# Splitting weight tiles of 2048 columns into halves of 1024 between ScalarE, VectorE and TensorE

## The chip, the cores and the metric

The kernel runs on one core of one Trainium2 chip. The metric is the device time of one execution in microseconds. Engines are named as the profile names them: PE is TensorE (PEld its weight loads), DVE is VectorE, ACT is ScalarE, POOL is GpSimd and SP is SyncE.

## The reference

Two transformer-like blocks run one after the other, in f32, for one sequence of 512 tokens with D = 2048 (the first block has two layers, with a second stream of 256 context tokens). Cut to what matters here, every layer is a chain of products of the activations with large weight matrices, and smaller work between them:

```python
hl = xl * (1.0 + sc_l) + sh_l                 # modulation, from silu(c) @ w_mod
parts = jnp.split(hl @ w_in[l], SPLIT_POINTS) # 2048 x 8192
y = concat(short_conv(...), diff_attention(...), multiscale_pool(...))
x = layernorm(ALPHA * x + gate * (y @ w_out[l]))
# second block: the same frame, with
y_attn = banded_sink_attention(q, k, v, ...) * silu(g_attn)
u = glu_a * sigmoid(glu_b)                    # then a causal depthwise conv of 31 taps
y_conv = (silu(layer_norm(u)) @ w_pw + b_pw) * silu(g_conv)
```

## The kernel before, in words

**Weight tiles.** All large products are cut into 296 weight tiles. A tile holds the 128 output columns that one PSUM bank receives, for all 2048 inputs: in SBUF it is 128 partitions x 2048 columns, of which each block of 128 columns is one stationary operand. The tiles are numbered through the whole program (`j`), and the list `STREAM` gives their order: for the context tokens `cconv`, `chead`, `cpool`, `cout` (tiles 0 to 71, 256 tokens), for the main tokens `aconv` to `aout` (72 to 143, 512 tokens), `kv1` (144 to 159, 256 tokens), `bconv` to `bout` (160 to 231), then the second block: `glu` (232 to 255), `kv2`, `attn2`, `pw`, `out2` (to 295), with 512 tokens.

**Three terms.** An f32 product is made of three passes: the weights and the activations are each split in a rounded part and a rest (`hi`, `lo`), and PE adds hi*hi + hi*lo + lo*hi. So a tile takes 48 matmuls (lines 946 to 948 in `product`, 16 blocks of 128 inputs times 3).

**The path of one tile.** SP loads `raw` (1 MB) when the rest of tile j-2 is written (`load`, line 350, waits for `lo_done`). ACT copies it rounded to `w_hi` (`hi`, line 542; the instruction is recorded at the helper's line 540) when the load has landed and PE has finished tile j-2 (`tile_done`). DVE writes `w_lo` = `raw` - `w_hi` (`lo`, line 1270, instruction at line 1274). PE waits for `lo_done` at the head of `weight_tile` (line 951). `raw`, `w_hi` and `w_lo` hold two tiles each, by the parity of j, and there are two PSUM banks for results (`acc`, freed by `acc_free`).

**The order on each engine** is written out by hand. ACT's stream in every stage is: `hi(j + 1)`, then the eviction of tile j when PE has finished it. So `hi(j + 1)` always stands behind the eviction of tile j-1. DVE's stream is: `lo(j + 1)`, then the stage's own work on earlier results. That work is small in some stages and large in others: in `aconv` and `bconv` DVE also multiplies modulation weights of the next layer (`mod_tiles`, line 1321) whose tiles POOL loads, in `aconv` and `kv1` it finishes the layer norm of the stage before (lines 1586, 1594, 1605, 1611), and in `glu` and `kv2` it computes the 31 taps of the depthwise convolution (`taps`, line 1731, instruction at 1739), about 10 taps behind each `lo`. At the head of each stage ACT and DVE first make the activations' `h_hi` and `h_lo`; PE follows block by block through the stage's first tile (`split_before`), and the second tile's `hi` stands behind that work on ACT.

**A tile in two results.** In `pw` a weight tile holds two products of 8 blocks each; the first signalled `pw_done`, the second `tile_done`.

`shown(sem, n)` gives the value of a semaphore when n events have happened, counting what it was granted at the start; `At` is a linear expression in the loop's counter.

Of the kernel before, what the change touches and what calls it, by code (L numbers as in the profile page):

```python
# [8 lines left out]
F32 = mybir.dt.float32  # L9
F32R = mybir.dt.float32r  # L10
ALU = mybir.AluOpType
# [4 lines left out]
D = 2048  # L16
KT = D // P
# [91 lines left out]
def build(nc, A, out):  # L109
    with ExitStack() as ctx:  # L110
        def sb(name, cols, dt=F32, rows=P):
            return ctx.enter_context(nc.sbuf_tensor(name, [rows, cols], dt))

        def psum(name, cols):
            return ctx.enter_context(nc.psum_tensor(name, [P, cols], F32))
# [3 lines left out]
        def sem(name, credit=0):  # L119
            s = ctx.enter_context(nc.semaphore(name))  # L120
            credits[id(s)] = credit
            return s
# [5 lines left out]
        raw = sb("raw", 2 * D)  # L128
        w_hi = sb("w_hi", 2 * D, F32R)
        w_lo = sb("w_lo", 2 * D, F32R)  # L130
# [25 lines left out]
        acc = [psum(f"acc{n}", 512) for n in range(2)]  # L156
# [25 lines left out]
        m0_used = sem("m0_used", 4)  # L182
        m0_row = sem("m0_row", 2)
        m0_cols = sem("m0_cols", 2)
        raw_landed = [sem(f"raw_landed{n}") for n in range(2)]
        hi_done = sem("hi_done")
        lo_done = sem("lo_done", 2)
        tile_done = sem("tile_done", 2)
        acc_free = sem("acc_free", 2)
        mraw_landed = [sem(f"mraw_landed{n}") for n in range(2)]  # L190
        gate0_landed = [sem(f"gate0_landed{n}") for n in range(4)]
# [23 lines left out]
        s_ready = sem("s_ready", 4)  # L215
# [3 lines left out]
        t_done = sem("t_done", 1)  # L219
        at_evac = sem("at_evac", 4)  # L220
        pv_done = sem("pv_done", 1)
# [5 lines left out]
        vt_done = sem("vt_done", 1)  # L227
# [10 lines left out]
        sq_used = sem("sq_used", 4)  # L238
# [15 lines left out]
        pv2_done = sem("pv2_done", 1)  # L254
        u2_ready = sem("u2_ready", 2)
        th_done = sem("th_done")
        pw_done = sem("pw_done")
        ypw_done = sem("ypw_done", 2)
        pool_done = sem("pool_done", 1)
        y2_done = sem("y2_done", 1)  # L260
# [3 lines left out]
        def shown(s, n):  # L264

            n = (n if isinstance(n, At) else At(n)) + credits[id(s)]
            assert n.c > 0 or n.k, "a wait for nothing"
            return n.val

        def grant(eng, *sems):  # L270

            for s in sems:
                eng.sem_inc(s, credits[id(s)])
# [36 lines left out]
        def loop(eng, first, last, body):  # L310
            with eng.Fori(first, last) as i:
# [6 lines left out]
        H_AT = {"c.h": 0, "c.y": 16, "a.h": 32, "a.y": 48, "kv1": 64, "b.h": 80, "b.y": 96, "g.h": 112,  # L318
                "pw": 128, "g.y": 136}
# [28 lines left out]
        @block.sync  # L348
        def _(sp):
            def load(j, src):  # L350
                sp.wait_ge(lo_done, shown(lo_done, j - 1))
                sp.dma_start(raw[:, j.odd * D:(j.odd + 1) * D], src).then_inc(raw_landed[j.odd], 16)

            def stream(phase, w, t0):
                n_iter, tiles = {n: (i, t) for n, i, t in STREAM}[phase]

                def body(i):
                    for p in range(tiles):
                        load(j_at(phase, i, p), w[bass.ds(i * tiles + (t0 + p), 1)])
                if n_iter == 1:  # L360
                    body(0)
                else:
                    loop(sp, 0, n_iter, body)

            def mod0(i):
                for s in range(4):
                    sp.wait_ge(m0_used, shown(m0_used, At(s - 3, 4, i)))
                    sp.dma_start(xy[:, s * D:(s + 1) * D].rearrange("p (t n) -> p t n", t=2),
                                 A["wm"][bass.ds(i * 8 + 2 * s, 2)].rearrange("t p n -> p t n")).then_inc(m0_landed[s], 16)
            loop(sp, 0, MOD0_CHUNKS, mod0)  # L370
            w0, w1, w2 = A["w0"], A["w1"], A["w2"]
            for c in "ca":
                for phase, t0 in (("conv", 0), ("head", 16), ("pool", 48), ("out", 56)):
                    stream(c + phase, w0, t0)

            def kv(i):
                for p, t in ((0, 18), (1, 17)):
                    load(j_at("kv1", i, p), w1[bass.ds(i * 4 + t, 1)])
            loop(sp, 0, N_HEADS, kv)
            for phase, t0 in (("conv", 0), ("head", 16), ("pool", 48), ("out", 56)):  # L380
                stream("b" + phase, w1, t0)
            at = 0
            for phase in ("glu", "kv2", "attn2", "pw", "out2"):
                stream(phase, w2, at)
                n, i, t = [s for s in STREAM if s[0] == phase][0]
                at += i * t
# [151 lines left out]
        def _(act):  # L538
            def f(out, in_, func=ACT.Copy, **kw):
                return nc.scalar.activation(out, in_, func, **kw)  # L540

            def hi(j):

                act.wait_ge(raw_landed[j.odd], shown(raw_landed[j.odd], j.half.times(16) + 16))
                act.wait_ge(tile_done, shown(tile_done, j - 1))
                f(w_hi[:, j.odd * D:(j.odd + 1) * D], raw[:, j.odd * D:(j.odd + 1) * D]).then_inc(hi_done, 1)

            def modulate(c, src, T, scale, bias, first=0, last=KT, normed=None):

# [292 lines left out]
            for p in range(4):  # L842
                j, a = j_at("kv2", 0, p), a_at("kv2", 0, p)
# [63 lines left out]
            def pw(i):  # L907
                for t in range(2):
                    j = j_at("pw", i, t)
                    hi(j + 1)  # L910
                    for s in range(2):
                        m = 2 * t + s
                        a = a_at("pw", i, m)
                        act.wait_ge(dve_phase, shown(dve_phase, after("attn2")))
                        act.wait_ge(ypw_done, shown(ypw_done, At(m - 1, 4, i)))
                        if s == 0:
                            act.wait_ge(pw_done, shown(pw_done, At(t + 1, 2, i)))
                        else:
                            act.wait_ge(tile_done, shown(tile_done, j + 1))
                        f(ev[s][:], acc[a.odd][:, :], ACT.Identity,  # L920
                          bias=vec("b_pw", i * 4 + m)).then_inc(acc_free, 1)
# [11 lines left out]
        def _(pe):  # L933
            mm = nc.tensor.matmul

            def product(o, j, ks, w_k0=0, split_before=None, beside=None):

                for n, k in enumerate(ks):
                    if beside is not None and n == 3:
                        beside()  # L940
                    if split_before is not None:
                        pe.wait_ge(hlo_done, shown(hlo_done, split_before + k + 1))
                    w = slice(j.odd * D + (w_k0 + n) * P, j.odd * D + (w_k0 + n + 1) * P)
                    T = o.shape[1]
                    x = slice(k * SEQ, k * SEQ + T)
                    mm(o, w_hi[:, w], h_hi[:, x], start=n == 0, stop=False)  # L946
                    mm(o, w_hi[:, w], h_lo[:, x], start=False, stop=False)  # L947
                    last = mm(o, w_lo[:, w], h_hi[:, x], start=False, stop=n == len(ks) - 1)  # L948
                return last

            def weight_tile(j, a, T, h, first=False, beside=None):

                pe.wait_ge(lo_done, shown(lo_done, j + 1))
                pe.wait_ge(acc_free, shown(acc_free, a - 1))
                product(acc[a.odd][:, 0:T], j, range(KT), split_before=h if first else None,
                        beside=beside).then_inc(tile_done, 1)
# [166 lines left out]
                pe.wait_ge(sqsum_ready, shown(sqsum_ready, LN_NO[c] + 1))  # L1123
                mm(pv[:, 0:T], ones[:], norm_buffers(c)[1][:, 0:T], start=True, stop=True).then_inc(sq_used, 1)

            grant(pe, m0_used, m0_cols, tile_done, s_ready, t_done, pv_done, vt_done, sq_used, pv2_done)
            pe.wait_ge(setup_dve, shown(setup_dve, 1))

            def mod0_chunk(i, s):
# [64 lines left out]
            for v in range(2):  # L1194
                pe.wait_ge(acc_free, shown(acc_free, a_at("kv2", 0, 2 + v) + 1))
                pe.wait_ge(vt_evac, shown(vt_evac, VT0["kv2"] + v))
                for b in range(4):
                    last = nc.tensor.transpose(misc[:, P * b:P * (b + 1)], ev[3 - 2 * v][:, P * b:P * (b + 1)], ident[:])
# [46 lines left out]
            def pw(i):  # L1245
                for t in range(2):
                    j = j_at("pw", i, t)
                    pe.wait_ge(lo_done, shown(lo_done, j + 1))
                    for s in range(2):
                        a = a_at("pw", i, 2 * t + s)  # L1250
                        pe.wait_ge(acc_free, shown(acc_free, a - 1))
                        product(acc[a.odd][:, :], j, range(8), 8 * s, H_AT["pw"]).then_inc((pw_done, tile_done)[s], 1)
            loop(pe, 0, 2, pw)
            project_out("g", "out2")
            mean("g", SEQ)
# [4 lines left out]
        def _(dve):  # L1260
            tt, ts, stt = nc.vector.tensor_tensor, nc.vector.tensor_scalar, nc.vector.scalar_tensor_tensor
# [7 lines left out]

            def lo(j):  # L1270

                dve.wait_ge(hi_done, shown(hi_done, j + 1))
                s = slice(j.odd * D, (j.odd + 1) * D)
                tt(w_lo[:, s], raw[:, s], w_hi[:, s].bitcast(F32), ALU.subtract).then_inc(lo_done, 1)  # L1274

            def modulated(c, T, i):

# [363 lines left out]
            for l in range(DEPTH):  # L1641
                tt(lam[:, l:l + 1], small[:, 5 + 2 * l:6 + 2 * l], small[:, 4 + 2 * l:5 + 2 * l], ALU.subtract)
                s = vec(f"subln{l}")
# [4 lines left out]
            for name in ("cln_g", "cln_b"):  # L1648
                s = vec(name, 0, 8)
# [323 lines left out]
```

## Time and profile before

| what | value |
|---|---|
| time, median of 3 runs | 3728.88 us (3725.71 to 3730.09) |
| the profiled execution: span from its first to its last instruction | 3719.5 us |
| the profiled execution's own run time beside its span | not given; the span is 9.4 us below the median of the runs |
| PE busy | 3467.2 us, 93% |
| DVE busy | 2288.1 us, 62% |
| ACT busy | 1303.7 us, 35% |
| POOL busy | 209.9 us, 6% |

How to read it: the median covers the whole execution, the span only the stretch between instructions. A busy share is a mean over stages with different limits. Matmuls overlap their successors, so that a PE that is always busy still starts a matmul only every so often; the distance between two starts is what a matmul costs.

### The profile page before, as it was taken

Reading aid. Unit: us, or ns where it says so; the run is one execution under the profiler, and the core shown is the slowest. Engines: PE = TensorE matmul, PEld = TensorE weight load, DVE = VectorE, ACT = ScalarE, POOL = GpSimd, SP = SyncE. Lnnn points to the kernel's source line nnn. Section 1 sums busy time; section 2 is a strip of 40 time slices with the busy share of each in tenths; the row PEclk is TensorE's granted clock in tenths of the full one; section 3 lists DMA queues with packets and bytes.
Section 4 is the critical chain, followed back from the end, with each engine's and each line's share of the span. In section 5 each row is a group of like instructions: output and inputs, shape, how many; then the busy total and the mean of one; then the engine's idle time right before and its main releaser. Section 6 shows DMA issues by size and latency. Waiting matters only on the chain.

```text
span 3719.5 us, 48605 instructions
## 1 busy us (share of the span) xinstructions
PE 3467.2 (93%) x16800; PEld 2732.9 (73%) x16800; DVE 2288.1 (62%) x2909; ACT 1303.7 (35%) x1730; POOL 209.9 (6%) x396
## 2 busy tenths in 40 slices
PE   8699999899999999999799999999997998898996
PEld 2299989678777777878588777767785777687784
DVE  6455565886767764656655566665655888554433
ACT  0145544432334343225522334342326222344323
POOL 1000000000000000110000000000110000000000
PEclk9799999999999999998899999999998999999998
DMA  9844445445223222654554222221652222221231
GB/s 379 267 169 168 166 157 218 143 176 189 105 85 111 99 84 81 234 195 152 187 192 161 105 95 107 104 83 71 217 201 91 80 90 85 80 79 62 103 115 65
DMA packets 95158, 516.21 MB, mean 139 GB/s; under 512 B 11536, under 2 KB 11568, under 8 KB 55760
## 3 DMA queue, kind: packets, MB, share of 16 engines
q1 hardware_dynamic: 51328, 343.95, 25.4%
q0 software_dynamic: 43728, 170.91, 13.3%
q8 instruction: 63, 1.03, 0.1%
q14 instruction: 39, 0.32, 0.0%
HBM read 492.80 MB, written 22.02 MB: 138 GB/s over the span
## 4 chain that ended last, share of the span: by engine, by line
PE 72%; DVE 10%; issue 6%; DVEq 4%; DMA 4%; ACT 3%; ACTq 1%; POOL 0%; SPq 0%; POOLq 0%; PEldq 0%
PE acc L946 20%; PE acc L947 19%; PE acc L948 19%; DVE xy L1739 5%; PE S L1007 3%; PE pv L1041 2%; DVEq L1738 2%; PE S L1136 2%; DVE w_lo L1274 1%; PE misc L1118 1%; PE S L1015 1%; DMA bias_d<-evt 1%; PE S L1009 1%; DMA xy<-in_wm 1%; DVE gates L1321 1%
## 5 line engine op out<-in xcount | busy, mean ns | idle before, releaser
L946 PE MATMUL acc<-h_hi,w_hi 128*128 128x512 f32 (+1 forms) x4736 | 1747.3, 369 | 142.5 <-DVE h_lo L1280 67.6
L947 PE MATMUL acc<-h_lo,w_hi 128*128 128x512 f32 (+1 forms) x4736 | 1713.4, 362 | 0.0
L948 PE MATMUL acc<-h_hi,w_lo 128*128 128x512 f32 (+1 forms) x4736 | 1711.8, 361 | 0.0
L946 PEld LDWEIGHTS acc<-h_hi,w_hi 128*128 128x128 f32 x4736 | 908.5, 192 | 337.4 <-issue 126.2
L948 PEld LDWEIGHTS acc<-h_hi,w_lo 128*128 128x128 f32 x4736 | 909.4, 192 | 135.3
L947 PEld LDWEIGHTS acc<-h_lo,w_hi 128*128 128x128 f32 x4736 | 910.5, 192 | 132.0 <-issue 6.3
L1274 DVE TENSOR_TENSOR w_lo<-raw,w_hi 128x2048 fp32r<-128x2048 f32 x296 | 677.0, 2288 | 270.9 <-ACT w_hi L540 266.0
L540 ACT ACTIVATE w_hi<-raw 128x2048 fp32r<-128x2048 f32 x296 | 564.7, 1908 | 6.9 <-DVEq L1265 6.2
L540 ACT ACTIVATE ev<-acc 128x512 f32<-128x512 f32 (+1 forms) x210 | 110.8, 532 | 1255.9 <-PE acc L948 1222.7
L1321 DVE SCALAR_TENSOR_TENSOR gates<-gates,csil 128x512 f32<-128x512 f32 x568 | 412.2, 750 | 82.8 <-DMA gates<-in_wm 48.1
L1423 DVE TENSOR_REDUCE small<-S 128x2 f32<-128x1536 f32 (+1 forms) x80 | 123.4, 1543 | 309.7 <-PE S L1009 304.4
L1739 DVE SCALAR_TENSOR_TENSOR xy<-work,vecs,xy 128x512 f32 (+1 forms) x240 | 180.4, 752 | 36.3 <-issue 31.7
L540 ACT ACTIVATE ev<-acc,modc 128x512 f32<-128x512 f32 (+1 forms) x64 | 40.7, 635 | 452.7 <-PE acc L948 452.7
L400 POOL DMA_DIRECT2D gates<-in_wm x192 | 101.7, 530 | 1134.3 <-DVE gates L1321 1016.9
L540 ACT ACTIVATE work<-S,small 128x768 f32<-128x768 f32 (+1 forms) x160 | 129.1, 813 | 73.2 <-DVE small L1423 73.1
L1007 PE MATMUL S<-kb,qb 64*128 64x512 f32 (+1 forms) x320 | 134.9, 598 | 0.0
L1136 PE MATMUL S<-xy,csil 128*2 128x512 f32 x256 | 116.2, 609 | 16.7 <-DVEq L1626 8.6
L1041 PE MATMUL pv<-work,vtok 128*128 128x512 f32 (+1 forms) x224 | 94.9, 569 | 18.6 <-ACT work L540 18.6
L1136 PEld LDWEIGHTS S<-xy,csil 128*2 128x2 f32 x256 | 20.9, 86 | 105.3 <-issue 81.3
L1551 DVE SCALAR_TENSOR_TENSOR xy<-qb,ev 128x512 f32 (+2 forms) x32 | 20.0, 625 | 124.9 <-ACT ev L540 120.6
L1551 DVE SCALAR_TENSOR_TENSOR xy<-kb,ev 128x512 f32 (+2 forms) x32 | 20.0, 626 | 121.6 <-ACT ev L540 121.6
L1041 PEld LDWEIGHTS pv<-work,vtok 128*128 128x128 f32 x224 | 40.7, 190 | 61.1 <-issue 48.6
(199 smaller groups left out, 2160.2 us busy)
## 6 DMA issues: line engine op xcount, KB each, us to landing
raw<-in_w SPq DMA_DIRECT2D x296, 1024.0 KB, 4.8
gates<-in_wm POOLq DMA_DIRECT2D x216, 512.0 KB, 4.4
xy<-in_wm SPq DMA_DIRECT2D x32, 1024.0 KB, 10.0
x_d<-xy POOLq DMA_DIRECT2D x2, 4096.0 KB, 14.0
vtok<-in_wm POOLq DMA_DIRECT2D x8, 512.0 KB, 7.2
qb<-x_d POOLq DMA_DIRECT2D x16, 256.0 KB, 3.1
kb<-x_d POOLq DMA_DIRECT2D x16, 256.0 KB, 3.8
out_y<-xy POOLq DMA_DIRECT2D x4, 1024.0 KB, 4.1
```

The lines of the kernel that those rows point to most:

```text
L400: pool.dma_start(mraw[:, m.odd * MOD_KT * MC:(m.odd + 1) * MOD_KT * MC], A["wm"][bass.ds(i * per + (first + t), 1)]).then_inc(mraw_landed[ ...
L540: return nc.scalar.activation(out, in_, func, **kw)
L946: mm(o, w_hi[:, w], h_hi[:, x], start=n == 0, stop=False)
L947: mm(o, w_hi[:, w], h_lo[:, x], start=False, stop=False)
L948: last = mm(o, w_lo[:, w], h_hi[:, x], start=False, stop=n == len(ks) - 1)
L1007: last = mm(S[:, 1024 * m:1024 * m + T], q, kb[h, 0:T], start=True, stop=True)
L1041: last = mm(pv[:, 0:T], vtok[:, P * k:P * (k + 1)], a_t[:, k * T:(k + 1) * T], start=k == 0, stop=k == NK // P - 1)
L1136: last = mm(S[0:2, MC * s:MC * (s + 1)], csil[:, k:k + 17:16], xy[:, slot * D + n * MC:slot * D + (n + 1) * MC], start=k == 0, stop=k == K ...
L1274: tt(w_lo[:, s], raw[:, s], w_hi[:, s].bitcast(F32), ALU.subtract).then_inc(lo_done, 1)
L1321: last = ts(s, x, cc, None, ALU.mult) if k == 0 else stt(s, x, cc, s, ALU.mult, ALU.add)
L1423: nc.vector.tensor_reduce(small[:, 0:2], S3[:, :, 0:NK], AX_X, ALU.max, negate=True).then_inc(nb_ready, 1)
L1739: stt(u, work[:, tap:tap + SEQ], vec("dw", c * TAPS + tap), u, ALU.mult, ALU.add)
```

## The change

Every weight tile is handled in two halves of 1024 columns (8 blocks of 128 inputs) by ACT, DVE and PE, each half with its own count on `hi_done` and `lo_done`. The load stays one transfer of 1 MB. PE counts `half_done` on the 24th matmul of a tile, and waits for `lo_done` at the head of each half. `pw_done` goes, since `half_done` says the same.

```diff
-        lo_done = sem("lo_done", 2)
+        lo_done = sem("lo_done", 4)
         tile_done = sem("tile_done", 2)
+        half_done = sem("half_done", 2)
...
-                sp.wait_ge(lo_done, shown(lo_done, j - 1))
+                sp.wait_ge(lo_done, shown(lo_done, (j - 1).times(2)))
...
             def hi(j):
                 act.wait_ge(raw_landed[j.odd], shown(raw_landed[j.odd], j.half.times(16) + 16))
-                act.wait_ge(tile_done, shown(tile_done, j - 1))
-                f(w_hi[:, j.odd * D:(j.odd + 1) * D], raw[:, j.odd * D:(j.odd + 1) * D]).then_inc(hi_done, 1)
+                for h in range(2):
+                    used = (half_done, tile_done)[h]
+                    act.wait_ge(used, shown(used, j - 1))
+                    s = slice(j.odd * D + h * D // 2, j.odd * D + (h + 1) * D // 2)
+                    f(w_hi[:, s], raw[:, s]).then_inc(hi_done, 1)
...
             def product(o, j, ks, w_k0=0, split_before=None, beside=None):
                 for n, k in enumerate(ks):
+                    if (w_k0 + n) % (KT // 2) == 0:
+                        pe.wait_ge(lo_done, shown(lo_done, j.times(2) + (1 + (w_k0 + n) // (KT // 2))))
...
                     last = mm(o, w_lo[:, w], h_hi[:, x], start=False, stop=n == len(ks) - 1)
+                    if w_k0 + n == KT // 2 - 1:
+                        last.then_inc(half_done, 1)
...
             def weight_tile(j, a, T, h, first=False, beside=None):
-                pe.wait_ge(lo_done, shown(lo_done, j + 1))
                 pe.wait_ge(acc_free, shown(acc_free, a - 1))
...
             def lo(j):
-                dve.wait_ge(hi_done, shown(hi_done, j + 1))
-                s = slice(j.odd * D, (j.odd + 1) * D)
-                tt(w_lo[:, s], raw[:, s], w_hi[:, s].bitcast(F32), ALU.subtract).then_inc(lo_done, 1)
+                for h in range(2):
+                    dve.wait_ge(hi_done, shown(hi_done, j.times(2) + (h + 1)))
+                    s = slice(j.odd * D + h * D // 2, j.odd * D + (h + 1) * D // 2)
+                    tt(w_lo[:, s], raw[:, s], w_hi[:, s].bitcast(F32), ALU.subtract).then_inc(lo_done, 1)
```

## Rows read from the trace of the kernel before

**Rows 1.** The page: span, busy shares, and the groups of lines 1274 and 540.

```profile
span 3719.5 us, 48605 instructions
PE 3467.2 (93%) x16800; PEld 2732.9 (73%) x16800; DVE 2288.1 (62%) x2909; ACT 1303.7 (35%) x1730; POOL 209.9 (6%) x396
...
L1274 DVE TENSOR_TENSOR w_lo<-raw,w_hi 128x2048 fp32r<-128x2048 f32 x296 | 677.0, 2288 | 270.9 <-ACT w_hi L540 266.0
L540 ACT ACTIVATE w_hi<-raw 128x2048 fp32r<-128x2048 f32 x296 | 564.7, 1908 | 6.9 <-DVEq L1265 6.2
```

**Rows 2.** The waits, whole span: who waited for whom, us in total, times, longest.

```profile
PE acc L946 <- DVE w_lo L1274: 59.8, 35, 6.2
```

**Rows 3.** Timeline of PE in out2 (start, us taken), across a tile boundary.

```profile
3578.69 0.39 PE L948 MATMUL acc<-h_hi,w_lo 128*128 128x512 f32 x1
3578.92 0.39 PE L946 MATMUL acc<-h_hi,w_hi 128*128 128x512 f32 x1
3579.15 0.39 PE L947 MATMUL acc<-h_lo,w_hi 128*128 128x512 f32 x1
```

**Rows 4.** Timelines of ACT, DVE and PE at the last tiles of kv1; ACT's first from apool.

```profile
1485.71 6.34 ACT L540 ACTIVATE h_hi<-xy  x12
...
1775.82 4.91 DVE L1611 TENSOR_TENSOR xy<-xy,t 128x512 f32 x8 [0.30 <-issue]
1776.78 5.75 ACT L540 ACTIVATE xy<-xy,vecs  x8 [1.38 <-DVE xy L1611]
1782.44 1.89 ACT L540 ACTIVATE w_hi<-raw 128x2048 fp32r<-128x2048 f32 x1
1784.23 0.36 ACT L540 ACTIVATE ev<-acc 128x256 f32<-128x256 f32 x1
1784.36 4.49 DVE L1274 TENSOR_TENSOR w_lo<-raw,w_hi 128x2048 fp32r<-128x2048 f32 x2 [3.63 <-ACT w_hi L540]
1786.78 0.57 PE L946 MATMUL acc<-h_hi,w_hi 128*128 128x256 f32 x1 [6.17 <-DVE w_lo L1274]
1788.77 4.90 DVE L1611 TENSOR_TENSOR xy<-xy,t 128x512 f32 x8
```

**Rows 5.** Timeline of PE: first matmuls of tiles 1, 145, 148, 161 and 233.

```profile
193.06 0.38 PE L946 MATMUL acc<-h_hi,w_hi 128*128 128x256 f32 x1 [2.46 <-DVE w_lo L1274]
1691.11 0.58 PE L946 MATMUL acc<-h_hi,w_hi 128*128 128x256 f32 x1 [2.42 <-DVE w_lo L1274]
1712.39 0.36 PE L946 MATMUL acc<-h_hi,w_hi 128*128 128x256 f32 x1 [1.23 <-DVE w_lo L1274]
1828.14 0.49 PE L946 MATMUL acc<-h_hi,w_hi 128*128 128x512 f32 x1 [3.81 <-DVE w_lo L1274]
2843.11 0.79 PE L946 MATMUL acc<-h_hi,w_hi 128*128 128x512 f32 x1 [2.51 <-DVE w_lo L1274]
```

**Rows 6.** The waits of PE, stretch 2880 to 3150 us (glu and kv2).

```profile
PE acc L946 <- DVE w_lo L1274: 22.6, 14, 2.8
```

**Rows 7.** Groups of DVE, stretch 2880 to 3150 us.

```profile
L1739 DVE SCALAR_TENSOR_TENSOR xy<-work,vecs,xy 128x512 f32 (+1 forms) x221 | 166.1, 752 | 34.8 <-issue 31.7
L1274 DVE TENSOR_TENSOR w_lo<-raw,w_hi 128x2048 fp32r<-128x2048 f32 x22 | 50.2, 2284 | 0.0
```

**Rows 8.** The waits of PE, stretch 665 to 850 us (aconv).

```profile
PE acc L946 <- DVE w_lo L1274: 13.2, 8, 4.4
```

**Rows 9.** The waits of PE, stretch 1685 to 1800 us (kv1).

```profile
PE acc L946 <- DVE w_lo L1274: 12.1, 5, 6.2
```

**Rows 10.** Timeline of DVE: the splits of tiles 81, 145 (with 146) and 233.

```profile
790.48 2.29 DVE L1274 TENSOR_TENSOR w_lo<-raw,w_hi 128x2048 fp32r<-128x2048 f32 x1 [3.35 <-ACT w_hi L540]
1688.68 4.64 DVE L1274 TENSOR_TENSOR w_lo<-raw,w_hi 128x2048 fp32r<-128x2048 f32 x2
2840.68 2.29 DVE L1274 TENSOR_TENSOR w_lo<-raw,w_hi 128x2048 fp32r<-128x2048 f32 x1 [0.36 <-ACT w_hi L540]
```

**Rows 11.** Busy time by stretch, and PEclk (granted clock), in glu's second tile.

```profile
2843.00:2846.00 3.00, 2.89 (x7) 2.32 (x8) 0.00 (x0) 3.00 (x5) 0.00 (x0) 0.50 0.55 210
```

## What the change will do to the time, predicted before it ran

> **What bounds the kernel.** I read the page first. PE is busy 93% of the span, and the two instructions that the change touches, one of 2288 ns on DVE and one of 1908 ns on ACT, come 296 times each [rows 1]. Most of DVE's idle time before `w_lo` ends with ACT's `w_hi`: the two are a chain, not two loads. So I looked next for what PE waits for, since only that can be won. Over the whole span PE waited 59.8 us, in 35 places, for `w_lo` to come [rows 2]. The other 261 tiles start without such a wait. Then I looked at a tile boundary in a stage with nothing else to do: 3578.69 is the last matmul of one tile, 3578.92 the first of the next, 3579.15 the second [rows 3]. The distance is 0.23 us inside and across. Two waits with computed values and one increment stand at that boundary and cost nothing, so where PE has its data a tile takes its 48 starts and no more, and the change can give nothing.
>
> Last I asked for each of the 35 places what made `w_lo` late, since there are two answers with different prices. Either the chain is late (ACT reached `hi` late; the DVE row then has a wait for ACT's `w_hi`, as in [rows 4]), or DVE is late (busy with its own stage; no bracket on the row of line 1274).
>
> **The price of a half.** On DVE, two splits of 2048 columns start at 1784.36 and the next instruction at 1788.77 [rows 4]: 2.205 us from start to start, against 2.29 from start to end, so 0.08 us of each overlaps the next. Eight instructions of 512 columns take 4.91 us [rows 4]: (4.91 - 0.08) / 8 = 0.603 each. From these two sizes 1024 columns occupy 0.603 + 1.602 / 3 = 1.137 us and end 1.22 us after their start. Two halves occupy 2.274 us instead of 2.205: DVE pays **0.07 us a tile**. On ACT, `w_hi` starts at 1782.44 and its successor at 1784.23: 1.79 us, 1.91 to its end. Twelve instructions of 512 columns take 6.34 us, 0.52 each [rows 4]. So a half occupies 0.52 + 1.27 / 3 = 0.94 us and ends after 1.06; ACT pays 0.09 us a tile.
>
> **What PE wins where the chain is late.** Before: 1.89 + 0.03 + 2.29 = 4.21 us from the start of `hi` to the end of `lo`. After: the first half of `w_lo` is there after 1.06 + 0.03 + 1.22 = 2.31 us. PE starts **1.90 us** earlier. DVE starts the second half at 1.09 + 1.14 = 2.23 us and ends it at 3.45, so DVE itself is free **0.76 us** earlier. PE asks for the second half 24 matmuls after its start (24 x 0.23 = 5.5 us, and about half of that with 256 tokens), and it comes 1.14 us after the first: no wait in the middle.
>
> **What PE wins where DVE is late.** The first half ends 2.29 - 1.22 = **1.07 us** earlier, if DVE starts at the same time; DVE itself comes out 0.07 us later.
>
> **The earlier release wins nothing by itself.** `hi(j + 1)` stands behind the eviction of tile j-1 on ACT, which waits for the whole of tile j-1. When ACT reaches it, `half_done` has long come. The loads keep their trigger, the end of both halves.
>
> Now the places, in order of time. An idle time in brackets is counted from the modelled end of the matmul before (0.39 us), while the next could start after 0.23 [rows 3]; so what can be won is 0.16 us more than the bracket.
>
> - `cconv`, tile 1: PE waits 2.46 us [rows 5], the chain is late. **-1.9**. From there the stage follows PE.
> - `aconv` [rows 8]: 13.2 us in 8 waits, but DVE is what is full here, so what counts is DVE's own time. At tile 81 DVE waits 3.35 us for `w_hi` [rows 10], behind the layer norm on ACT; there is one more such place, four tiles before. Each gives DVE 0.76 us. Eight other splits cost 0.07 each. At the last wait PE has 1.07 on top: 1.52 - 0.56 + 1.07 = **-2.0**.
> - `kv1` [rows 9]: 12.1 us in 5 waits. Tile 145 waits 2.42 [rows 5], but DVE goes into this split without waiting for ACT [rows 10], so it wins 1.07. Tile 148 waits 1.23 [rows 5], and tile 152 the same: DVE's split before was late by the chain (0.76) and this one is late by DVE (1.07), which is more than the wait, so 1.4 each. Tile 159 waits 6.17 [rows 4]: the split before it hands 0.76 through the layer norm (DVE line 1611, ACT `xy`, `w_hi`), then 1.90. What tile 157 wins is not added, since 159 waits for that chain and not for PE. 1.07 + 2.8 + 2.66 = **-6.5**.
> - `bconv`, tile 161: waits 3.81 [rows 5], the chain is late. **-1.9**.
> - The head of `glu`, tile 233: waits 2.51 [rows 5], but DVE was free only 0.36 us before it started [rows 10], so 0.36 + 1.07 = 1.4, less 0.1 for one more ACT half ahead of the layer norm, whose store the taps wait for. **-1.3**.
> - `glu` and `kv2` afterwards [rows 6, 7]: 22.6 us of waits in 14 places, of which nothing comes back. DVE is full: taps of 166.1 us with 34.8 idle between them, and 22 splits of 50.2 us with 0.0 idle before them, are 251 of 270 us. PE would start each tile 1.07 us earlier against DVE, and then wait that much longer for the next. DVE pays for one more split at the end, 23 x 0.07: **+1.6**.
> - The rest of the 59.8: 59.8 - 22.6 - 13.2 - 12.1 - 2.46 - 3.81 - 2.51 = 3.1 us in 5 short waits (`chead`, `cout`, `aout`, `bpool`). All are shorter than 1.07, so they go: 3.1 + 5 x 0.16 = **-3.9**.
>
> Sum: -1.9 - 2.0 - 6.5 - 1.9 - 1.3 + 1.6 - 3.9 = **-15.9 us**.
>
> To this comes the clock. Behind the wait of tile 233 PE ran with a granted clock of 0.50 [rows 11], the lower of its two levels, 1.2 and not 2.4 GHz; before, it had idled for 2.5 us. Three us at half speed are 1.5 us of work. Tiles 1, 161 and 233 have such waits and become shorter by 1.4 to 1.9 us. Whether the clock then stays up I can't tell: between nothing and 3 x 1.5 = 4.5 us. I take one of the three, **-1.5**.
>
> Where a satisfied wait and an increment stand in the middle of a tile, the trace of before has no row in a long tile of that form. The bounds: nothing, as at the boundary [rows 3], or the overlap of two matmuls, 0.39 - 0.23 = 0.16 us a tile, if the wait let the array run empty. I take nothing, since the boundary has the same kinds of instruction.
>
> The Trainium skill says otherwise of the increment: in "TensorE: Matmul & The Clock Gate", section "The cost: per-tile semaphore tail", increments on completion serialize at some 26 ns each. The boundary with its increment shows no such cost; by the page it would be an estimated 260 x 0.026 = 6.8 us, and the time 3718.
>
> Small costs that I set at nothing: ACT's 0.09 and DVE's 0.07 us in the head stages, `attn2`, `out2`. DVE and ACT wait for PE there; without that cover they would be 250 x 0.07 = 17 us.
>
> So -15.9 - 1.5 = -17.4 us. The sum is made on a span of 3719.5 us, which becomes 3702.1. The runs' median lies 9.4 us above that span, and I carry this over: 3728.9 - 17.4 = 3711.5, say **3711**.
>
> **The rivals.**
>
> *A: the wait in the middle stops PE (slower).* If PE drains at the new wait, each tile that PE bounds (296 less the 36 that wait anyhow, 260) pays 0.16 us: +42 us, and the time is 3728.9 - 17.4 + 42 = 3753. From 0.067 us a tile on it eats the gain, from 0.096 on the kernel is measurably slower. For it: there is a register value to compute in the loops. Against it: the boundary. 0.07.
>
> *B: the added increment costs a tenth of a distance.* 0.023 us a tile, which [rows 3] with their two decimals only just exclude at the boundary: +6 us, 3717. 0.08.
>
> *C: the waits were not the last to end.* If behind `w_lo` other things are due (`h_lo` at stage heads, the modulation loads in `aconv`, the store before the taps), only the plain places win: `cconv`, `bconv` and the last of `kv1`, 1.9 + 1.9 + 2.7, less 1.6 and a DVE price that could be higher. If each second half pays the gap that taps have between them (34.8 / 221 = 0.16 us [rows 7]), that is 23 x 0.16 = 3.7 more. Then -6.5 + 1.6 + 3.7 = -1.2 us: 3728. 0.15.
>
> *D: more than the sum.* All three clock stretches go (-4.5), and some more where PE's idle time after a short stage step stands at no matmul in the waits: 3705. 0.10.
>
> **How the numbers follow.** The forecast of 3711 has 0.60. Leaving out A and most of C, the range is 3703 (D, and 2 us for the runs' scatter) to 3723. About 0.2% (7.5 us) is what a measurement of this kernel can tell from no change. Forecast, B and D are faster by more: 0.78. C is 0.15. A is 0.07.
>
> **What the profile after will show.** Line 1274's successor 592 times with about 1220 ns, ACT's `w_hi` 592 times with about 1060. Across the middle of a tile PE's starts stay 0.23 us apart (A and B say otherwise). PE's waits for `w_lo` fall from 59.8 to about 42, nearly all in `aconv`, `glu` and at tiles 159 and 161. Tile 1 starts 1.9 us earlier. The stretch from the store to the end of `kv2` is 1.6 us longer. It is wrong if a wait for `w_lo` shows in the middle of tiles, if DVE's pair of halves takes more than 2.4 us, or if tile 159 comes less than 2.6 us sooner after tile 157's eviction than before.

## The result

| what | value |
|---|---|
| time before, median of 4 runs | 3729.49 us (3725.71 to 3732.84) |
| time after, median of 4 runs | 3700.95 us (3699.21 to 3703.37) |
| ratio | 0.9928, 95% interval 0.9914 to 0.9942 |
| the profiled execution of after | span 3698.3 us, own time 3699.87 us, mean granted clock 0.969 |

The change makes the kernel 28.5 us faster. I had predicted 17.4 us less than before, 3711 us, with a range from 3703 to 3723: the sign was right, and the time lies 2 us below the range. Among all executions of the experiments below, a single one, of the kernel before, took 6959 us; nothing on record says why, and no interval counts it.

**The profile after.** The page, the rows that answer to [rows 1] (in groups: busy us, mean ns | idle before):

```profile
span 3698.3 us, 49778 instructions
...
PE 3469.1 (94%) x16800; PEld 2735.4 (74%) x16800; DVE 2302.7 (62%) x3205; ACT 1331.3 (36%) x2026; POOL 210.8 (6%) x396
...
L1282 DVE TENSOR_TENSOR w_lo<-raw,w_hi 128x1024 fp32r<-128x1024 f32 x592 | 696.8, 1219 | 199.4 <-ACT w_hi L540 195.9
L540 ACT ACTIVATE w_hi<-raw 128x1024 fp32r<-128x1024 f32 x592 | 591.7, 1051 | 7.4 <-DVEq L1272 6.2
```

The prices of the halves are the predicted ones: 1219 ns on DVE (1220 forecast) and 1051 on ACT (1060). DVE's busy time for the splits grew by 696.8 - 677.0 = 19.8 us, 0.067 a tile. DVE's idle time before them fell by 71 us, of which 70 are time in which it had waited for ACT.

The waits of PE for `w_lo`, over the whole span, in `kv1` and in `glu` with `kv2`, against [rows 2, 9 and 6]:

```profile
PE acc L951 <- DVE w_lo L1282: 42.1, 20, 4.6
```

```profile
PE acc L951 <- DVE w_lo L1282: 6.4, 2, 4.6
```

```profile
PE acc L951 <- DVE w_lo L1282: 18.5, 8, 2.9
```

59.8 us in 35 places became 42.1 in 20; about 42 was forecast. The timeline of PE in `out2`, across the middle of a tile, where the new wait and the new increment stand (the second row is the 24th matmul, the third the 25th), and then the first matmuls of tiles 1, 145, 148, 161 and 233, against [rows 5]:

```profile
3564.58 0.39 PE L952 MATMUL acc<-h_lo,w_hi 128*128 128x512 f32 x1
3564.80 0.39 PE L953 MATMUL acc<-h_hi,w_lo 128*128 128x512 f32 x1
3565.03 0.39 PE L951 MATMUL acc<-h_hi,w_hi 128*128 128x512 f32 x1
3565.26 0.39 PE L952 MATMUL acc<-h_lo,w_hi 128*128 128x512 f32 x1
```

```profile
193.08 0.58 PE L951 MATMUL acc<-h_hi,w_hi 128*128 128x256 f32 x1 [0.46 <-DVE w_lo L1282]
1685.32 0.39 PE L951 MATMUL acc<-h_hi,w_hi 128*128 128x256 f32 x1 [1.75 <-DVE w_lo L1282]
1703.05 0.36 PE L951 MATMUL acc<-h_hi,w_hi 128*128 128x256 f32 x1
1812.88 0.49 PE L951 MATMUL acc<-h_hi,w_hi 128*128 128x512 f32 x1 [1.81 <-DVE w_lo L1282]
2826.13 0.50 PE L951 MATMUL acc<-h_hi,w_hi 128*128 128x512 f32 x1 [1.08 <-DVE w_lo L1282]
```

In the middle of a tile the starts stay 0.23 us apart. The distance there is no longer than inside the halves in 291 of the 296 tiles; in the other five, the first tiles of `cconv`, `aconv`, `kv1`, `bconv` and `glu`, PE follows the split of the activations. The waits are shorter by 2.00 us at tiles 1 and 161, where the chain was late (1.90 forecast), by 0.7 to 1.4 at tiles 145 and 233, and gone at tile 148. At the end of `kv1` the chain itself can be read, against [rows 4]:

```profile
1770.83 1.99 ACT L540 ACTIVATE w_hi<-raw 128x1024 fp32r<-128x1024 f32 x2
...
1771.89 4.63 DVE L1282 TENSOR_TENSOR w_lo<-raw,w_hi 128x1024 fp32r<-128x1024 f32 x4 [2.78 <-ACT w_hi L540]
...
1773.17 0.58 PE L951 MATMUL acc<-h_hi,w_hi 128*128 128x256 f32 x1 [4.64 <-DVE w_lo L1282]
```

From the start of `w_hi` to PE's first matmul it is now 1773.17 - 1770.83 = 2.34 us; before it was 1786.78 - 1782.44 = 4.34. DVE's row holds the four halves of two tiles: 4.63 = 3 x 1.137 + 1.22, so the halves follow each other without a gap. In no tile of this profile does DVE's second half start more than 1.144 us after the first.

**Where the 28.5 us are.** The two profiled spans differ by only 3719.5 - 3698.3 = 21.2 us. That was the first open question: 7.3 us of the gain are in the runs and not in the two profiles. The second: 1.6 us lie outside the span of after, where I had carried over 9.4.

### The profile page after: what moved, and what is told of

Its sections match the earlier page's. It is cut to its first block, busy times and chain, and to the rows that moved or that the text cites. A ratio compares the mean times of both kernels' runs of the same rounds, so it can differ in the third digit from the quotient of the medians.

```text
span 3698.3 us, 49778 instructions
## 1 busy us (share of the span) xinstructions
PE 3469.1 (94%) x16800; PEld 2735.4 (74%) x16800; DVE 2302.7 (62%) x3205; ACT 1331.3 (36%) x2026; POOL 210.8 (6%) x396
## 3 DMA queue, kind: packets, MB, share of 16 engines
q8 instruction: 64, 1.05, 0.1%
## 4 chain that ended last, share of the span: by engine, by line
PE 77%; DVE 10%; DVEq 3%; DMA 3%; issue 3%; ACT 3%; ACTq 1%; SPq 0%; POOL 0%; POOLq 0%; PEldq 0%
PE acc L951 21%; PE acc L953 21%; PE acc L952 21%; DVE xy L1747 5%; PE S L1013 3%; PE pv L1047 3%; PE S L1142 2%; DVE w_lo L1282 1%; DVEq L1746 1%; PE S L1021 1%; PE misc L1124 1%; PE S L1015 1%; DMA bias_d<-evt 1%; DMA xy<-in_wm 1%; DVE gates L1329 1%
## 5 line engine op out<-in xcount | busy, mean ns | idle before, releaser
L1282 DVE TENSOR_TENSOR w_lo<-raw,w_hi 128x1024 fp32r<-128x1024 f32 x592 | 696.8, 1219 | 199.4 <-ACT w_hi L540 195.9
L540 ACT ACTIVATE w_hi<-raw 128x1024 fp32r<-128x1024 f32 x592 | 591.7, 1051 | 7.4 <-DVEq L1272 6.2
```

## The experiments

The kernel before ran beside the others each time; its median was 3728.53 us in the first four experiments (21 runs, one chip) and 3728.71 in the last four (10 runs, another chip). "Slower" or "faster than the changed kernel" is counted from the 3699.98 us of after again. All times are medians; an interval is that of the ratio.

### The kernel before, and the changed one, once more

No edit. What was expected:

> The kernel before, once more, for the spans and clocks of its runs. Of the 28.5 us between the medians only 21.2 are between the two profiled spans, and after's span lies 1.6 us below its own run's time where I had carried 9.4 us over for before. Theory S: about 1.6 us lies outside the span in before too, and its profiled execution was a short one; then the spans of these runs lie at 3724 to 3731, their times 1.6 us above them, and they show more low clock than the profiled execution. Rival O: before has some 9 us outside its span; then the spans lie near 3719 and the times near 3729.

> The changed kernel once more, beside the kernel before on the same chip: ratio 0.992 to 0.993 (27 to 29 us), if the first result holds. The step from time to span stays 1.6 us.

Before again: 3728.92 us, ratio 1.0001 (0.9992 to 1.001). The long execution is one of its eleven; without it the median is 3728.69. After again: 3699.98 us, ratio 0.9924 (0.9911 to 0.9938), 28.5 us as the first time. The spans settle the first question. The profiled one of before again is

```profile
core 0: 3728.0 us, clock 0.968
```

and its own time 3729.59, 1.6 us more. The spans of the 21 runs of before beside it go from 3722.3 to 3732.2 us (median 3726.5), with 1.6 us outside them in the median; the granted clock was 0.968 or less in 17 of them. So theory S holds and rival O falls: the execution that I read, with a span of 3719.5 us and a clock of 0.970, was shorter than every one of them.

With two pairs of profiles the gain can be split by place. I compare the start of each tile on PE, and take how the difference between the two kernels grows from one place to the next. The columns are two different pairs of executions; `kv1` is counted from tile 144 to 160 without the tiles 145 and 159 themselves, which stand in the row of the clock:

| stretch | predicted | before, after | both again | 
|---|---|---|---|
| wait of tile 1 | -1.9 | -2.0 | -2.0 |
| tile 3 to the end of `cout` | part of -3.9 | -3.6 | -3.9 |
| `apool`, `aout` | part of -3.9 | -1.6 | -1.4 |
| `bconv` (from tile 163) to `bout` | part of -3.9 | -0.3 | -0.8 |
| `aconv` | -2.0 | -0.7 | -2.2 |
| waits in `kv1` (145, 148, 152, 157, 159) | -6.5 | -7.0 | -7.0 |
| wait of tile 161 | -1.9 | -2.0 | -2.0 |
| wait of tile 233 | -1.3 | -1.4 | -1.4 |
| tile 234 to the end of `kv2` | +1.6 | -0.8 | -0.8 |
| `attn2` | 0 | -0.7 | -3.3 |
| duration of tiles 1 and 2, 145, 159, 161 and 162, 233 (clock) | -1.5 | -3.6 | -5.6 |
| `ahead` | 0 | +1.8 | +1.3 |
| `pw`, `out2` | 0 | +0.5 | +1.5 |
| sum from tile 0 to the last matmul | -17.4 | -21.3 | -27.6 |

At the listed waits for `w_lo` (tiles 1, 161, 233 and `kv1`) the two pairs agree to 0.05 us with each other, and with the forecast to 0.1 us, in `kv1` to 0.5. The pairs differ most in `aconv`, in `attn2` and in the row of the clock.

### PE's marks alone

The kernel before, whole weights, with PE's new instructions (the wait that stood at the head of `weight_tile` goes; the one below stands at the head and in the middle of each tile):

```diff
             def product(o, j, ks, w_k0=0, split_before=None, beside=None):
                 for n, k in enumerate(ks):
+                    if (w_k0 + n) % (KT // 2) == 0:
+                        pe.wait_ge(lo_done, shown(lo_done, j + 1))
...
+                    if w_k0 + n == KT // 2 - 1:
+                        last.then_inc(half_done, 1)
```

> The kernel before with PE's new instructions only: in the middle of each tile a second wait that is already satisfied, and half_done counted on the 24th matmul; the weights stay whole. Theory: no difference (within 2 us of the kernel before), as at the tile boundary. Rival A (PE drains at the wait): +0.16 us a tile, +42 us. Rival B (the increment costs a tenth of a start's distance): +6 us.

3728.83 us, ratio 1.0001 (0.9991 to 1.001). 296 more waits and 292 more increments (in `pw` the new one takes the place of `pw_done`) cost 0.3 us together, which is less than the measurement can tell. Rivals A (+42 us) and B (+6) fall. In the trace the starts across the middle of a tile are 0.23 apart:

```profile
3590.43 0.39 PE L950 MATMUL acc<-h_hi,w_lo 128*128 128x512 f32 x1
3590.66 0.39 PE L948 MATMUL acc<-h_hi,w_hi 128*128 128x512 f32 x1
3590.88 0.39 PE L949 MATMUL acc<-h_lo,w_hi 128*128 128x512 f32 x1
```

The rule of the Trainium skill that I had weighed ("TensorE: Matmul & The Clock Gate", "The cost: per-tile semaphore tail", some 26 ns for an increment) would have given an estimated 292 x 0.026 = 7.6 us. No such cost is here: the upper end of the interval, 1.001, is 3.7 us. One increment in 48 matmuls of a running stream isn't on the path.

### PE late, and ACT whole: the two halves of the gain

The changed kernel, but PE waits for both halves before the tile:

```diff
                     if (w_k0 + n) % (KT // 2) == 0:
-                        pe.wait_ge(lo_done, shown(lo_done, j.times(2) + (1 + (w_k0 + n) // (KT // 2))))
+                        pe.wait_ge(lo_done, shown(lo_done, j.times(2) + 2))
```

> ACT and DVE work in halves as in the change, but PE waits for both halves of w_lo before a tile. Theory (the gain is PE's earlier start: 1.90 us where the chain is late, 1.07 where DVE is late): only the overlap of ACT with DVE stays, 0.76 us where the chain is late, and DVE late costs 0.07. By place: tile 1 -0.8, aconv -1.0, kv1 -2.9, tile 161 -0.8, tile 233 -0.3, glu and kv2 +1.6, the short waits -1, the clock -0.5: -5.5 us from the kernel before, so 3724. Rival (the overlap alone brings it, PE's early start only moves waits): within 4 us of the changed kernel, 3701 to 3705.

3713.62 us, ratio 0.9962 (0.9948 to 0.9976): 14.9 us faster than before, and 13.6 slower than the changed kernel. Neither theory gave that. By place, against before again, the theory's prices stand at single waits: tile 1 -0.85 (-0.8 expected), tile 161 -0.87 (-0.8), tile 233 -0.29 (-0.3); tiles 144 to 160 with their clock gave -3.8 (-2.9). `aconv` gave -3.2 where -1.0 was expected. What the list lacked are places: -2.75 us between tile 3 and the end of `cout`, -3.5 in `attn2`, and the clock behind tile 161 (-1.6). So the price of a wait was right, and the list of places and the clock's term were short.

The changed kernel, but ACT writes `w_hi` whole:

```diff
-                for h in range(2):
-                    used = (half_done, tile_done)[h]
-                    act.wait_ge(used, shown(used, j - 1))
-                    s = slice(j.odd * D + h * D // 2, j.odd * D + (h + 1) * D // 2)
-                    f(w_hi[:, s], raw[:, s]).then_inc(hi_done, 1)
+                act.wait_ge(tile_done, shown(tile_done, j - 1))
+                s = slice(j.odd * D, (j.odd + 1) * D)
+                f(w_hi[:, s], raw[:, s]).then_inc(hi_done, 2)
```

> The changed kernel, but ACT writes w_hi whole; DVE and PE keep their halves. Theory: where the chain is late PE's first half comes 1.89 + 0.03 + 1.22 = 3.14 us after the start of hi, not 2.31, and DVE is free 0.83 us later. By place, from the steps between the changed kernel and the one before: tile 1 +0.8, head of chead +0.8, cpool and cout +1.5, aconv +0.8, tiles 145 to 159 +2.4, tile 161 +0.9, tile 233 +0.4, attn2 +0.7: +8 us, 3708. Rival (only PE's wait for a half of w_lo matters, ACT's halves cost 0.09 us a tile for nothing): 3700 or below.

3714.15 us, ratio 0.9963 (0.9951 to 0.9975): 14.2 us slower than the changed kernel, where 8 were expected. From tile 0 to the last matmul its profile is 8.6 us longer than that of after again: tile 1 +0.85, tile 3 to `cout` +2.9, `aconv` +1.3, `kv1` +3.0, tile 161 +0.85, tile 233 +0.28, `attn2` +1.5, and 2.1 less in all other stretches together. The rest of the difference of the two profiles, 4.9 us, lies before tile 0 (3.2, where no weight tile is at work) and after the last matmul (1.7). Of the 14.2 us between the medians the places thus give 8.6, as expected; the rest I can't place. The rival falls: taking away ACT's halves costs as much (14.2 us) as taking away PE's early start (13.6).

**The places that my list lacked.** I had listed the places by one row of the waits, PE for `w_lo`. But PE also waits for other work of DVE that stands behind the split. In `cpool` it is a short product of `work` into `pv` in the middle of the stage. The waits of PE for that work, whole span, before again and after again (lines 1075 and 1523 of the kernel before are 1081 and 1531 of the changed one):

```profile
PE pv L1075 <- DVEq L1523: 9.8, 4, 3.8
```

```profile
PE pv L1081 <- DVEq L1531: 8.7, 3, 4.0
```

And why DVE comes to it sooner, DVE's timeline at tile 55, before again and after again:

```profile
547.83 2.29 DVE L1274 TENSOR_TENSOR w_lo<-raw,w_hi 128x2048 fp32r<-128x2048 f32 x1 [4.67 <-ACT w_hi L540]
550.04 0.28 DVE L1507 COPY work<-ev 128x256 f32<-128x256 f32 x1
```

```profile
541.30 2.36 DVE L1282 TENSOR_TENSOR w_lo<-raw,w_hi 128x1024 fp32r<-128x1024 f32 x2 [4.62 <-ACT w_hi L540]
543.58 0.29 DVE L1515 COPY work<-ev 128x256 f32<-128x256 f32 x1
```

Both splits start when ACT's output is there. ACT began `w_hi` at 545.90 in before again and at 540.22 in after again, so `COPY`, DVE's next work, comes 4.14 us after that start with whole weights and 3.36 with halves: 0.78 us, the 0.76 that I had worked out for a late chain. Tile 55 then starts 0.78 us earlier. It is the same price, at a place where PE's rows name neither `w_lo` nor line 1274. `attn2`, which I had put at nothing, has a smaller place of this kind: tile 263 starts 3.92 us behind tile 262's last matmul before, 3.21 after and 3.20 with PE late; PE waits there for DVE's `work`.

### `w_lo` whole where DVE bounds

The changed kernel, with one instruction of 2048 columns in `lo` for `glu` after its first six tiles and for `kv2` (in `glu`: `whole=not first`, in `kv2`: `whole=True`):

```diff
-            def lo(j):
+            def lo(j, whole=False):
+                if whole:
+                    dve.wait_ge(hi_done, shown(hi_done, j.times(2) + 2))
+                    s = slice(j.odd * D, (j.odd + 1) * D)
+                    tt(w_lo[:, s], raw[:, s], w_hi[:, s].bitcast(F32), ALU.subtract).then_inc(lo_done, 2)
+                    return
```

> The changed kernel, but DVE writes w_lo whole (2048 columns in one instruction, two counts) for the tiles of glu after its first six and of kv2. Theory (DVE bounds this stretch, a pair of halves costs 0.07 us more than a whole, PE's earlier start only makes it wait longer): 22 x 0.07 = 1.5 us faster than the changed kernel, 3698.5. Rival (in this stretch too PE's 1.07 us earlier start lets the evictions end earlier, which DVE waits for): slower than the changed kernel, by up to 3 us.

3698.74 us, ratio 0.9918 (0.9904 to 0.9931). That is 1.2 us less than after again, in the direction and near the size of the theory, but the two intervals overlap nearly wholly, so it isn't shown by the times. By place the stretch from tile 239 to the end of `kv2` is 1.4 us shorter than in after again, and 1.5 were expected. The profile is of an execution 6.8 us above the median of its kernel: the rest of its way from tile 0 to the last matmul is 5.8 us longer than in after again, 3.1 of it in `ahead`, where the edit changes nothing.

### Three pieces

Pieces of 512, 512 and 1024 columns, everywhere (`CUTS = (0, 512, 1024, 2048)`); SP waits for three counts a tile:

```diff
             def hi(j):
...
-                for h in range(2):
-                    used = (half_done, tile_done)[h]
-                    act.wait_ge(used, shown(used, j - 1))
-                    s = slice(j.odd * D + h * D // 2, j.odd * D + (h + 1) * D // 2)
+                for h in range(3):
+                    if h != 1:
+                        used = tile_done if h else half_done
+                        act.wait_ge(used, shown(used, j - 1))
+                    s = slice(j.odd * D + CUTS[h], j.odd * D + CUTS[h + 1])
...
             def product(o, j, ks, w_k0=0, split_before=None, beside=None):
...
-                    if (w_k0 + n) % (KT // 2) == 0:
-                        pe.wait_ge(lo_done, shown(lo_done, j.times(2) + (1 + (w_k0 + n) // (KT // 2))))
+                    if P * (w_k0 + n) in CUTS:
+                        pe.wait_ge(lo_done, shown(lo_done, j.times(3) + (1 + CUTS.index(P * (w_k0 + n)))))
```

> The changed kernel with three pieces of 512, 512 and 1024 columns in place of two of 1024, on ACT, DVE and PE. Theory: the first piece of w_lo is there 0.64 + 0.03 + 0.69 = 1.36 us after the start of hi, not 2.31, and with DVE late 0.53 us sooner; one more piece costs DVE another 0.07 us a tile. Chain late at tiles 1, 17, 57, 159, 161: -4.8; DVE late at 145, 148, 152, 157, 233: -2.7; glu and kv2 +1.6: -5.9 us from the changed kernel, 3694. Rival (the added instructions on ACT and DVE outweigh it, or PE now waits in the middle of tiles of 256 tokens): 3700 to 3705.

3693.50 us, ratio 0.991 (0.9896 to 0.9923): 35.2 us faster than before, and 6.5 us faster than the changed kernel where 5.9 were expected. The two intervals overlap by a little; four of the five runs, 3693.1 to 3695.4 us, lie below every one of the nine runs of the changed kernel (3698.48 us and more). By place against after again: tile 1 -0.65, tile 145 -0.54, tile 159 -1.05, tile 161 -0.94, tile 233 -0.54 (expected 0.95 where the chain is late, 0.53 where DVE is), tile 239 to the end of `kv2` +2.5 (+1.6 expected). At tile 1 no wait is left, which is why it gains less than 0.95. For tiles 148, 152 and 157 another 0.53 each had been expected, but that isn't there: tiles 152 and 157 gain nothing, and tile 148 comes 1.2 later behind tile 147, after a tile 145 that was 2.1 shorter in this profile by its clock. The first matmul of tile 161:

```profile
1810.34 0.50 PE L953 MATMUL acc<-h_hi,w_hi 128*128 128x512 f32 x1 [0.85 <-DVE w_lo L1284]
```

3.81 us of wait before [rows 5], 1.81 with halves, 0.85 with three pieces.

Last, the two together, three pieces and `w_lo` whole in `glu` and `kv2`:

> The three pieces of 512, 512 and 1024 columns, with w_lo written whole in glu after its first six tiles and in kv2. Theory: the sum of the two, 22 x 0.14 = 3.1 us faster than the three pieces everywhere: 3691. Rival as for the three pieces: no faster than the changed kernel.

3693.79 us, ratio 0.9906 (0.9891 to 0.9921). The stretch from tile 239 to the end of `kv2` is 3.9 us shorter than with three pieces everywhere (3.1 expected), and the whole from tile 0 to the last matmul 1.4 us: tile 145 is 2.2 us longer in it by low clock, of which 1.2 come back at tile 148, and `ahead` 1.6 longer. The median is the same, where 3.1 less were expected. Of these two the times don't say which is better. Both beat the kernel before and the changed one in their medians.

## Why the prediction was wrong in size

The gain was 28.5 us and the sum 17.4, which are 11.1 us too little. On the pair of executions that I read the sum lacks only 21.2 - 17.4 = 3.8 us; the other 7.3 are the base, which was an unusually short execution. Counted on a usual one (before again to after again, 27.6 us between tile 0 and the last matmul) the sum lacks 10.2: 4.1 in the row of the clock, 3.3 in `attn2`, 2.4 behind tile 234, 2.2 in the short waits and 1.0 in single places, less 2.8 that `ahead`, `pw` and `out2` took back. The steps one by one:

**The steps that held.** The prices of a half; PE's start 1.90 us earlier where the chain is late (2.0 at tiles 1 and 161); 1.07 where DVE is late (1.2 at tile 145); 1.4 at tile 148 and at tile 152 (1.48 and 1.50); 2.66 at tiles 157 and 159 together (2.77); 1.4 at tile 233 (1.42). The middle of a tile costs nothing (PE's marks alone). That the earlier release wins nothing by itself no run tried, but the traces show it: with whole weights, halves or three pieces, `w_hi` never starts less than 0.60 us after the start of the last matmul of the tile two before, so `half_done` never let ACT begin sooner. PE's waits fell to the 42 us named. Rivals A and B are refuted by the run with PE's marks alone, and C by the table: at the places of the sum the gain came, and each second half starts without a gap. D, more than the sum, is the one that came, and went further than the 3705 that I gave it.

**The step of the sum that failed first, "To this comes the clock ... I take one of the three, -1.5".** The mechanism was right and its size was not. In every profiled execution the following holds, as the time from the first to the last start in the tile (us) behind the distance that PE had stood before it:

| kernel | tile 73 | tile 161 | tile 233 |
|---|---|---|---|
| before | 12.44 behind 2.7 | 12.41 behind 4.2 | 12.18 behind 2.9 |
| before again | 12.39 behind 2.7 | 12.40 behind 4.2 | 12.29 behind 2.9 |
| PE's marks alone | 12.37 behind 2.8 | 12.40 behind 4.1 | 12.30 behind 2.8 |
| PE late | 12.25 behind 2.7 | 10.79 behind 3.3 | 12.17 behind 2.6 |
| ACT whole | 10.77 behind 1.7 | 10.79 behind 3.1 | 10.79 behind 1.8 |
| after | 10.78 behind 1.6 | 12.40 behind 2.2 | 10.79 behind 1.5 |
| after again | 10.76 behind 1.6 | 10.79 behind 2.2 | 10.78 behind 1.5 |
| `w_lo` whole in `glu` | 10.76 behind 1.6 | 10.80 behind 2.2 | 10.79 behind 1.5 |
| three pieces | 10.78 behind 1.1 | 10.80 behind 1.2 | 10.83 behind 1.0 |
| three pieces, whole in `glu` | 10.76 behind 1.1 | 10.79 behind 1.3 | 10.79 behind 1.0 |

With whole weights on both engines each of these tiles was 1.4 to 1.7 us longer, three times out of three. With halves or three pieces that was so in one of fifteen. The three together are 4.7 us, and tile 73, in `aconv`, wasn't on my list. Tile 1, which was, came out 0.5 and 1.5 us shorter. The rows for tile 233 are [rows 11] before and this one after (us, busy of PE, PEld, DVE, ACT, POOL, PEclk, DMA share, GB/s):

```profile
2826.13:2829.13 3.00, 3.00 (x13) 2.50 (x14) 1.08 (x1) 3.00 (x5) 0.00 (x0) 1.00 0.23 41
```

The granted clock is 1.00 where it was 0.50, and in the same 3 us 13 matmuls start where 7 did. The half speed of [rows 11] came in all three profiles with whole weights, which one execution couldn't tell me.

But the change also brought half speed where there had been none. At tiles 248, 251, 254 and 257, in `glu` and `kv2`, PE had stood 3.1 to 3.2 us ahead of the tile with whole weights, and they took 10.7 to 10.8 us in eleven of twelve cases. In six of the seven profiles with halves or three pieces it had stood 3.1 to 3.5 us, and they took 12.2 to 12.4 us every time; in the seventh, PE late, it had stood 3.3 us, and they took 10.8. So the length of the wait alone doesn't decide it there, and what does stays open. DVE bounds that stretch, and the first three cost nothing. The last one does: counted from tile 239, after is 1.2 us behind before at tile 257, which is 18 x 0.067, and 2.7 behind at tile 258, since tile 257 took 12.39 us and not 10.83. With PE late it is 1.3 at both.

**The second: the base.** "The sum is made on a span of 3719.5 us ... I carry this over." An offset of 9.4 us doesn't exist: 1.6 us are outside the span, and 7.8 are that this execution was shorter than usual. Against before again it was shorter by 3.8 us ahead of the first tile, by 2.7 at tiles 79 and 80, and by 1.6 at tiles 263 and 264. Most of the last two is low clock: tile 79 took 10.78 us in it, behind a distance of 1.9, and 12.41 in before again, behind 2.9; tile 263 took 10.75 and 11.71 (with PE's marks alone 11.76). After the change both took 10.77 or 10.78 us in both profiles. So a part of the gain was not in the trace that I read: at these tiles it had nothing to win back. It is most of what the two pairs of the table differ by: 1.5 us in `aconv`, 2.6 in `attn2` and 2.0 in the clock's row, of 6.3 in all. The 17.4 us belong to a short execution, and I took them from the time of a usual one. With the 1.6 us that are really outside the span, the forecast would have been 3702.1 + 1.6 = 3703.7.

**The third: the list of places.** "The rest of the 59.8 ... in 5 short waits, -3.9" took only rows that name `w_lo`. The stretches that belong to it gave 5.5 and 6.1 us. Of the difference 1.1 us lie at tiles 55 and 56, the end of `cpool` and the head of `cout`; tile 55 gains by what DVE does behind the split, as shown above. `attn2`, put at nothing, gave 0.7 and 3.3 us: 0.7 of it at tile 263 in the same way, the rest in the second pair alone, mostly low clock that the first one's before didn't have.

**The fourth: the store before the taps.** I had charged +1.6 for `glu` and `kv2` behind tile 234. From tile 239 on it was more, +2.8 and +2.6, by the half speed of tile 257. But between tiles 234 and 239 it was -3.5, since the taps began 2.4 us sooner against their store: POOL issues it and DVE waits for it. Before again and after again:

```profile
2871.34 0.54 POOL L448 DMA_DIRECT2D x_d<-xy  x1 [88.22 <-ACT xy L540]
...
2886.60 0.55 DVE L1736 TENSOR_SCALAR xy<-work,vecs 128x512 f32<-128x512 f32 x1 [6.65 <-DMA x_d<-xy]
```

```profile
2845.16 0.54 POOL L448 DMA_DIRECT2D x_d<-xy  x1 [86.24 <-ACT xy L540]
...
2858.04 0.55 DVE L1744 TENSOR_SCALAR xy<-work,vecs 128x512 f32<-128x512 f32 x1 [5.15 <-DMA x_d<-xy]
```

From the issue to the taps it is 15.3 us before and 12.9 after. In the three profiles with whole weights the store took 15.0 to 15.3 us from issue to landing, in the five with halves or three pieces 12.5 to 13.0, with PE late 14.5, with ACT whole 13.9. Two loads of `raw` run beside it, issued 1.3 us before and 8.8 us after it with whole weights, 2.2 before and 7.9 after it with halves. That they meet it at another point, once the clock and the waits ahead are gone, may be the cause, but it wasn't tried by itself, and it can't be all: PE late has the 2.2 and 7.9, and 14.5 us.

What stays open: the 1.3 to 1.8 us more in `ahead`. They lie in a stretch at half clock in a train of products just before tile 96. Five of the ten profiles have it, with whole weights (PE's marks alone) as well as with halves, and five have not. No part of the change goes with it that I could name; nor have I an account of the 5.6 us by which ACT whole cost more than its places.

## What to carry to other kernels

Price a change in a chain from two sizes of the same instruction, and split the places by what made each late: at the listed waits that came out within 0.1 us, over the five of `kv1` within 0.5. But list the places by the engine that comes free, not by the buffer that it writes: whoever waits for anything behind the shortened instruction gains too. Before you make a sum on one profiled execution, see where its own time stands among the runs. Where one of PE's waits is followed by half speed in several profiles, count that loss with the wait, since at three such tiles both went together here; and look for tiles that may fall to half speed by the change, as four did in `glu` and `kv2`.

## What I had not expected of the hardware

At the three tiles of the table the granted clock behind a wait went mostly by the length of the wait, but not only. The distance ahead of the tile was 2.6 us or more in thirteen cases, of which eleven were followed by half speed, and 2.2 us or less in seventeen, of which one was. So at tile 233 a distance that was cut from 2.9 to 1.5 us gave back 1.4 us of waiting and 1.5 of half speed behind it. Tiles 248, 251, 254 and 257, where distances of 3.1 to 3.3 us stood before full and before half speed, show that this is no rule for every place. The Trainium skill says of it that the same kernel has now more and now fewer slow matmuls, by how its start falls ("TensorE: Matmul & The Clock Gate", "Part 1: The HAM clock gate"), and the traces agree: tile 161 took 12.40 and 10.79 us in two executions of the changed kernel, both behind a distance of 2.2 us. The first 3 us of it in after and in after again, with a granted clock of 0.57 and of 1.00:

```profile
1812.88:1815.88 3.00, 3.00 (x8) 2.38 (x9) 2.83 (x4) 2.01 (x3) 0.00 (x0) 0.57 0.15 27
```

```profile
1814.31:1817.31 3.00, 3.00 (x13) 2.50 (x14) 2.83 (x4) 2.01 (x3) 0.00 (x0) 1.00 0.31 41
```

The start of the first tile scatters by 5.8 us between profiled executions, from 175.6 to 181.4 us, with hardly an edit ahead of it (before and before again, the same kernel, are 3.8 apart); a difference of two spans should leave it out.
